# RG-LRU gates of a two-layer hybrid decoder: each inner gate tile reads two input tiles instead of three, one of them put together by ScalarE from the halves of two neighbours

## The reference, cut to what matters

```python
xb = xf.reshape(B, L, LRU_BLOCKS, LRU_BLOCK)                      # 16 blocks of 80
r = sigmoid(einsum('blnc,ncd->blnd', xb, w_a).reshape(B, L, W) + b_a)
i = sigmoid(einsum('blnc,ncd->blnd', xb, w_x).reshape(B, L, W) + b_x)
log_a = -LRU_C * r * softplus(-lam)
a = exp(log_a)
u = sqrt(-expm1(2.0 * log_a)) * (i * xf)                          # then h_t = a_t h_{t-1} + u_t
lru_branch = (gelu(y_lru) * hl) @ w_lru_out
```

## Time and profile before

| what | value |
|---|---|
| median of 3 runs | 2459.19 us (2458.72 to 2462.03) |
| the profiled execution's own time | 2456.01 us |
| span of its trace | 2454.2 us |
| TensorE busy | 2423.3 us, 99% of the span |
| VectorE, ScalarE, GpSimd busy | 1178.2, 645.1, 1634.4 us |
| LRU steps of the first layer | from 511.4 to 678.6 us of the span |
| the same steps of the second layer | 1211.9 us later |

### The profile page before, as it was taken

How to read it: one execution, slowest core, us unless ns; L and a number is a source line. 1 busy time by engine, 2 the same in 40 slices (tenths; PEclk the granted TensorE clock), 3 DMA queues, 4 the chain that set the end, 5 groups by cost and what they waited for, 6 DMA issues and landing times.

```text
span 2454.2 us, 53114 instructions
## 1 busy us (share of the span) xinstructions
PE 2423.3 (99%) x19640; PEld 2364.6 (96%) x19640; DVE 1178.2 (48%) x1587; ACT 645.1 (26%) x982; POOL 1634.4 (67%) x1685
## 2 busy tenths in 40 slices
PE   8999999999999999999999999999999999999998
PEld 7999999999999999999999999999999999999998
DVE  8646363678644432022266373736786454211223
ACT  2404040446811211011114041413666112100111
POOL 6464646578887776776765555555888776667765
PEclk9999999999999999999999999999999999999999
DMA  5636363522232222322257373645223232223222
GB/s 209 237 121 244 121 241 117 206 87 91 85 102 92 95 90 81 104 90 83 94 166 250 114 250 120 239 133 190 88 91 90 97 95 91 90 82 103 91 85 88
DMA packets 121737, 315.51 MB, mean 129 GB/s; under 512 B 12192, under 2 KB 12960, under 8 KB 121568
## 3 DMA queue, kind: packets, MB, share of 16 engines
q1 hardware_dynamic: 60480, 199.78, 25.5%
q10 hardware_dynamic: 61088, 113.34, 13.0%
HBM read 272.69 MB, written 40.38 MB: 128 GB/s over the span
## 4 chain that ended last, share of the span: by engine, by line
PE 91%; DVE 4%; DVEq 2%; ACT 1%; issue 1%; DMA 0%; ACTq 0%
PE proj L370 55%; PE aux L370 27%; PE aux L625 2%; DVE scratch L1126 2%; PE aux L582 1%; PE aux L555 1%; PE proj L633 1%; PE aux L633 1%; DVEq L1129 1%; DVE scratch L1184 1%; PE aux L611 1%; PE proj L625 0%; DVEq L807 0%; DVEq L1160 0%; DVEq L1187 0%
## 5 line engine op out<-in xcount | busy, mean ns | idle before, releaser
L358 POOL TENSOR_TENSOR w_low<-w_raw,w_high 128x512 fp32r<-128x512 f32 x840 | 1091.1, 1299 | 124.5 <-issue 2.1
L356 POOL TENSOR_SCALAR w_high<-w_raw 128x512 fp32r<-128x512 f32 x840 | 549.7, 654 | 674.1 <-PE proj L370 495.4
L370 PE MATMUL proj<-x_high,w_high 128*128 128x260 f32 x2752 | 558.8, 284 | 11.4 <-DVE x_low L797 11.0
L370 PE MATMUL proj<-x_high,w_low 128*128 128x260 f32 x2752 | 555.0, 283 | 0.0
L370 PE MATMUL proj<-x_low,w_high 128*128 128x260 f32 x2752 | 554.1, 283 | 0.0
L370 PEld LDWEIGHTS proj<-x_high,w_high 128*128 128x128 f32 x2752 | 425.3, 189 | 20.6 <-issue 16.9
L370 PEld LDWEIGHTS proj<-x_high,w_low 128*128 128x128 f32 x2752 | 424.8, 189 | 0.0
L370 PEld LDWEIGHTS proj<-x_low,w_high 128*128 128x128 f32 x2752 | 424.0, 189 | 0.0
L370 PE MATMUL proj<-split_scratch,w_high 128*128 128x260 f32 x2544 | 409.2, 283 | 0.0
L370 PEld LDWEIGHTS proj<-split_scratch,w_high 128*128 128x128 f32 x2544 | 348.6, 188 | 5.0 <-issue 5.0
L370 PE MATMUL aux<-x_high,w_high 128*128 128x260 f32 x1344 | 270.9, 283 | 0.0
(11 more groups left out here) (197 smaller groups left out, 2283.5 us busy)
## 6 DMA issues: line engine op xcount, KB each, us to landing
w_raw<-in_wstream SPq DMA_DIRECT2D x252, 512.0 KB, 3.5
scratch<-in_sret ACTq DMA_DIRECT2D x96, 512.0 KB, 6.9
out_ret_s<-scratch ACTq DMA_DIRECT2D x64, 512.0 KB, 4.4
w_raw<-in_wstream SPq DMA_DIRECT2D x72, 448.0 KB, 3.3
w_raw<-in_wstream SPq DMA_DIRECT2D x48, 384.0 KB, 3.0
scratch<-v_rows ACTq DMA_DIRECT2D x64, 256.0 KB, 3.9
w_raw<-in_wstream SPq DMA_DIRECT2D x48, 320.0 KB, 2.9
out_ret_p<-scratch ACTq DMA_DIRECT2D x8, 512.0 KB, 5.5
```

What stands on the lines that cost most here:

```text
L356: pool.tensor_scalar(WH[:, j, w], WR[:, j, w], 1.0, 0.0, ALU.mult, ALU.add)
L358: pool.tensor_tensor(WL[:, j, w], WR[:, j, w], WH[:, j, w].bitcast(F32), ALU.subtract).then_inc(s["w_split"], 1)
L370: m = pe.matmul(out, wt[:, w, blk * P:(blk + 1) * P], x[xi], start=first and n == 0, stop=last and n == 2)
```

## The change

The inner gate tiles (`t` = 1, 2, 3) read of their two neighbours only rows 64 to 127 of the tile before and rows 0 to 63 of the tile behind. The new kernel copies these two halves into one mixed tile, high and low part each, so that `gates(g,t)` reads two tiles: its own and the mixed one. The weights are laid out to match, and the unit of these steps has 6 blocks instead of 7. ScalarE makes the copies, 64 partitions by 520 columns each, in two calls a tile: `mix_below` (two copies of the upper halves) and `mix_above` (two of the lower halves, then the semaphore `mix_full`, on which TensorE now waits as well). In addition, the sigmoids of step (1,0) move ahead of three other steps on ScalarE, and `read_y(1,0)` on VectorE ahead of `conv_low(1,3)` and `conv(1,4)`.

```diff
-BAND = [sorted({(b * BLK + e) // P for b in range(t * P // BLK, (t * P + P - 1) // BLK + 1)
-                for e in (0, BLK - 1)}) for t in range(GT)]
+LAST_READ = [sorted({(b * BLK + e) // P for b in range(t * P // BLK, (t * P + P - 1) // BLK + 1)
+                     for e in (0, BLK - 1)})[-1] for t in range(GT)]
+MIXED = range(1, GT - 1)
+LOWER, UPPER = slice(0, P // 2), slice(P // 2, P)
+BAND = [(0, 1)] + [(t, "mix") for t in MIXED] + [(GT - 2, GT - 1)]
...
+        MIX = [[GL[1][i][:, GT - 1 - t % 2, :] for i in range(2)] for t in range(GT)]
...
                     q = 0
-                    pe.wait_ge(s["xc_low"], layer * LT + (g * GT + BAND[t][-1] + 1))
+                    pe.wait_ge(s["xc_low"], layer * LT + (g * GT + LAST_READ[t] + 1))
+                    if t in MIXED:
+                        pe.wait_ge(s["mix_full"], layer * (GROUPS * len(MIXED)) + (g * len(MIXED) + t))
                     for w in range(2):
...
-                        q = spread(ub0, u, YG_UNIT[t], ring_begin(layer, n + w), XCH, XCL, BAND[t], q)
+                        outs = ring_begin(layer, n + w)
+                        for k in BAND[t]:
+                            if q in (0, CUT):
+                                unit_begin(ub0, u, q // CUT)
+                            hi, lo = MIX[t] if k == "mix" else (XCH[:, k, :], XCL[:, k, :])
+                            m = product(outs, u % 2, q, [(hi[:, c * HALF:(c + 1) * HALF], lo[:, c * HALF:(c + 1) * HALF])
+                                                         for c in range(2)], k == BAND[t][0], k == BAND[t][-1])
+                            q += 1
+                        m.then_inc(s["r_done"], 1)
...
                 conv(1, 3)
+                read_y(1, 0)
                 conv_low(1, 3)
                 conv(1, 4)
...
-                    read_y(1, t)
+                    if t:
+                        read_y(1, t)
...
+                def mix_below(g, t):
+
+                    if t >= 3:
+                        r_done(LRU_TILE["y", g, t - 2] + 1)
+                    act.wait_ge(s["xc_low"], layer * LT + (g * GT + t))
+                    for i, src in enumerate((XCH, XCL)):
+                        A(MIX[t][i][UPPER, :], src[UPPER, t - 1, :].bitcast(F32), copy)
+
+                def mix_above(g, t):
+
+                    act.wait_ge(s["xc_low"], layer * LT + (g * GT + t + 2))
+                    for i, src in enumerate((XCH, XCL)):
+                        m = A(MIX[t][i][LOWER, :], src[LOWER, t + 1, :].bitcast(F32), copy)
+                    m.then_inc(s["mix_full"], 1)
...
                     A(LA[:, b, :], LA[:, b, :], ACT.Tanh, scale=CUR[:, PC_SP + c:PC_SP + c + 1]
                       ).then_inc(s["th_full"], 1)
+                    if t + 1 in MIXED:
+                        mix_above(g, t + 1)
                     act.wait_ge(*freed(layer, n + 2))
...
                 first_tap(0, 2)
+                mix_below(0, 1)
                 for t in range(GT):
...
                     gated_high(0, t)
+                    if t + 2 in MIXED:
+                        mix_below(0, t + 2)
+                gate_sigmoids(1, 0)
                 conv_high(*FILL_X[GT - 1])
                 first_tap(1, 3)
                 conv_high(1, 3)
                 first_tap(1, 4)
+                mix_below(1, 1)
                 for t in range(GT):
-                    gate_sigmoids(1, t)
+                    if t:
+                        gate_sigmoids(1, t)
+                        if t + 1 in MIXED:
+                            mix_below(1, t + 1)
```

More of the change, by code:

```diff
@@ L42 @@
 BLK = LW // NBLK
-BAND = [sorted({(b * BLK + e) // P for b in range(t * P // BLK, (t * P + P - 1) // BLK + 1)
-                for e in (0, BLK - 1)}) for t in range(GT)]
+LAST_READ = [sorted({(b * BLK + e) // P for b in range(t * P // BLK, (t * P + P - 1) // BLK + 1)
+                     for e in (0, BLK - 1)})[-1] for t in range(GT)]
+MIXED = range(1, GT - 1)
+LOWER, UPPER = slice(0, P // 2), slice(P // 2, P)
+for t in range(GT):
+    for row in {b * BLK + e for b in range(t * P // BLK, (t * P + P - 1) // BLK + 1) for e in range(BLK)}:
+        assert row // P == t or t not in MIXED or (row // P, row % P < P // 2) in ((t + 1, True), (t - 1, False))
+BAND = [(0, 1)] + [(t, "mix") for t in MIXED] + [(GT - 2, GT - 1)]
 QK, GATES = 2 * KT, VT
@@ L252, in build @@
         AUX = ctx.enter_context(nc.psum_tensor("aux", [P, 4, 512], F32))
[L254 removed]
+        names = ("mix_full go_pool setup_ld boot w_split w_used p_done t_free r_done "
                  "rope_done qk_high qk_low qz_full st_high st_low aux_mm kv_high kv_low "
@@ L1674, in weight_units, with rows_of @@
     n = 0
+    def rows_of(r):
+        if isinstance(r, int):
+            return np.arange(r * P, (r + 1) * P)
+        above, below = (r[1] + 1) * P, (r[1] - 1) * P
+        return np.concatenate([np.arange(above, above + P // 2), np.arange(below + P // 2, below + P)])
     def tile(w, col, rows, put=0):
         for i, r in enumerate(rows):
-            out[n, :, (put + i) * P:(put + i + 1) * P] = w[r * P:(r + 1) * P, col:col + P]
+            out[n, :, (put + i) * P:(put + i + 1) * P] = w[rows_of(r), col:col + P]
     def spread(size, tiles):
@@ L1737, in y_gates @@
                 gates.append(full)
-            spread(YG_UNIT[t], [(full, t * P, BAND[t]) for full in gates]
+            spread(YG_UNIT[t], [(full, t * P, [(k, t) if k == "mix" else k for k in BAND[t]]) for full in gates]
                    + [(w_in[l], off[5] + g * wide + t * P, range(MT))])
```

1 line of the change is left out of this document (removed).

## The result

The changed kernel takes 2462.8 us in the median of 12 runs (2461.41 to 2468.73); the kernel before, run beside it, 2458.88 us (2454.38 to 2462.52). The ratio is 1.0017, with a 95% interval of 1.0009 to 1.0025. So it is slower by 3.9 us: more than the uncertainty of this comparison, and less than the 4.9 us that the prediction drew as its line. The prediction said 2464.8 us. So the direction came as forecast, and the size falls on the other side of the prediction's own line, where its rival "nothing to measure" stands.

The account below looks back on a forecast made before the run. TensorE, busy 99%, was taken as the bound, with a slackless ScalarE-VectorE ring behind it. Each layer 3.3 us later less 0.5 relief, two layers 5.6 us, on 2459.2 gives 2464.8 us; range 2454 to 2471.

Parts of the forecast that it names:

- nothing to measure: Rival, chance 0.32: whole time within 0.2% (4.9 us), through copy pairs at 0.55 us or more gain on VectorE.
- The work removed: TensorE, both layers: 24 blocks, 17.3 us, and sigmoid stops, 5.6 us, go; the gain if nothing else were late.
- The price of a copy: ScalarE: a pair of 64-partition copies takes 1.18 us and puts off what follows by about 1.1 us.
- Group 0: First group's LRU steps: copies make the ring 2.2 us late; TensorE waits 1.0 us at gates(0,2), 3.0 at gates(0,3).
- The ring: LRU steps: ScalarE and VectorE release each other in turn, 16.3 us a step against TensorE's 15.87, without slack.
- The relief: VectorE gains 0.5 us a layer from lighter GpSimd work, bounds 0 and 3 us.
- The ring has no slack to give it back: Steps (0,3) and (0,4) hold no delaying pair, yet the 2.2 us of lateness was to stay.
- The turn: Start of group 1: gates(1,1) waits 7 to 9 us for mix_above(1,1), starting at 623.8; floor without VectorE lateness 621.6.
- Group 1: Second group's steps: ScalarE needs 13.0 us against TensorE's 12.3; gates(1,3) starts at 650.2 with slow matmuls, before 645.49.
- The clock: TensorE at half clock for 18 matmuls after the 7 to 9 us stop at gates(1,1): 1.9 us charged.
- The sum: Whole kernel: each layer 3.3 us later less 0.5, so 2.8; two layers 5.6 us slower.
- Faster: the ring gets ahead of today: Rival, chance 0.14: VectorE's conv(1,4) ends 1.1 to 1.7 us earlier through 2 to 4 us relief; about 2452 us.

Follow-up runs that it names:

- the shorter ring: Gelu and its table load left out of the LRU steps, in the changed kernel (2446.07 us) and in the kernel before (2452.33 us).
- the slots first: Kernel before with the moved sigmoids and read_y, plus both read_out of step (1,0) ahead of one_less_a2(1,0) on VectorE; no copies: 2453.09 us.
- group 1's mixed tiles and the slot sooner: Mixed tiles in group 1 alone, read_out(1) ahead of one_less_a2(1,0), and read_out(0) moved ahead of conv_low(1,4): 2451.46 us.
- group 1 early: Changed kernel with group 1's mix_above calls made early, right behind mix_below; group 0 as in the change: 2457.66 us.
- the moves alone: Kernel before with only the moved sigmoids and read_y(1,0); gates still over three tiles, no copies: 2465.43 us.
- mixed tiles in group 1 alone: Changed kernel with group 0 back on three tiles, group 1's lower copies early, both read_out of step (1,0) ahead of one_less_a2(1,0): 2451.36 us.
- mixed tiles and the slots first: Changed kernel with group 1's lower copies early and both read_out of step (1,0) ahead of one_less_a2(1,0): 2451.09 us.

## Why the prediction came out right, and where its steps did not

**The work removed** (24 blocks of 0.721 us) is right: 144 matmuls are gone. The stop of 2.8 us is gone too, in both layers. The sentence "If nothing else were late, this would be the gain" hid the main thing: before the change TensorE had 0.7 us to spare at the slot of `y(1,1)`. The prediction tied this gain to the order on ScalarE alone and overlooked VectorE's; with no copies and no wait the time was 2456.96, not near 2436. For the changed kernel itself this did not matter, since there the wait for the copies comes first.

**The price of a copy** is right: 1.15 us a pair against 1.18, so 64 partitions cost what 128 do.

**Group 0.** Waits of 0.63 and 3.58 us against 1.0 and 3.0. The ring was late as said: from the start of the stage, 0.88 us later after than before, `conv_high` of tile (0,4) stands at 554.76 against 552.14, so 1.7 us late by itself (said 2.2).

**The relief is the term that was mis-sized.** "The ring has no slack to give it back" failed at once: the next `conv_high` stood at 570.67 against 569.76, level again. Windows of 10 us behind `gates(0,3)`, before and after (us, busy of PE, PEld, DVE, ACT, POOL, then granted clock, DMA, GB/s):

```profile
559.10:569.10 10.00, 10.00 (x86) 10.00 (x85) 9.55 (x10) 5.30 (x10) 8.73 (x8) 1.00 0.26 82
```
```profile
560.00:570.00 10.00, 9.94 (x61) 9.97 (x61) 6.63 (x11) 7.94 (x12) 4.91 (x5) 0.70 0.14 41
```

While TensorE stands and then runs slowly, GpSimd works 4.9 us instead of 8.7, and VectorE's share from L1182 (now L1202) to the end of the convolution took 570.58 - 563.89 = 6.7 us against 569.67 - 560.24 = 9.4. So one pass gave back 2.7 us, against 0.5 for a whole layer, and inside the bound of 3. By the turn the forecast's 2.2 us of lateness were -0.6 in the first layer and +1.2 in the second (below): relief of 2.8 and 1.0.

The two layers are each other's control here. Up to `gates(0,3)` every `conv_high` has the same place in both stages within 0.02 us, and both have the stop of 3.58 us there. Behind it 26 matmuls of the first layer ran at the granted clock of 0.50, and 15 of the second. The same 10 us in the second layer, and VectorE's share there:

```profile
1773.28:1783.28 10.00, 9.94 (x70) 9.97 (x71) 6.79 (x10) 7.57 (x12) 5.74 (x6) 0.83 0.13 39
```
```profile
1777.17 0.70 DVE L1202 TENSOR_TENSOR scratch<-scratch 128x520 f32<-128x520 f32 x1 [2.86 <-ACT scratch L1613]
...
1781.47 3.89 DVE L1146 SCALAR_TENSOR_TENSOR scratch<-scratch,params_cur 128x509 f32<-128x509 f32 x3
```

GpSimd worked 5.74 us instead of 4.91, and VectorE took 1785.36 - 1777.17 = 8.2 us instead of 6.7: the layer in which TensorE was slow for longer is 1.5 us ahead at the next `conv_high`. So the half pace in group 0 is part of the relief, a link that the prediction did not have. That GpSimd's rest is what speeds VectorE up is borne out by the 840 convolution instructions above; that it is all of it is not shown.

**The turn.** `conv_high(1,4)` was forecast near 618 and came at 616.50 (616.18 in the earlier trace rows, so 0.6 early by itself), and `gates(1,1)` at 621.79 against 623.8, after 2.69 us and not 7 to 9. Set back by the 0.88 us this is 620.9, just under the 621 that I had named as the point where I am wrong, and 0.7 below the floor that held without lateness. In the second layer, 2.24 us later at the start of its stage, `conv_high(1,4)` stands at 1831.58, 1.2 us late by itself (before: 1828.1), the wait is 5.64 us, and `gates(1,1)` starts at 1836.88. The mechanism is that of the forecast, the second layer near its size, the first at a third. The layers part at the half pace behind `gates(0,3)`, as shown; why the clock treated the same stop in two ways, no run shows.

**Group 1.** Waits of 0.77 and 0.72 us in the first layer (forecast 0.7 each, as 13.0 less 12.3). `gates(1,3)` starts at 648.15, with the offset taken off 1.8 us later than the earlier trace rows where 4.7 was said.

**The clock** fell, but elsewhere. Windows after, behind `gates(0,3)`, at the turn, and in the second layer's:

```profile
560.00:564.00 4.00, 3.94 (x18) 3.97 (x19) 0.93 (x4) 3.96 (x7) 1.14 (x2) 0.50 0.16 30
564.00:568.00 4.00, 4.00 (x28) 4.00 (x27) 3.78 (x7) 1.99 (x5) 1.77 (x2) 0.75 0.19 72
...
621.80:626.00 4.20, 4.20 (x35) 4.20 (x36) 2.23 (x5) 4.14 (x5) 1.76 (x3) 1.00 0.30 88
...
1836.00:1840.00 4.00, 3.12 (x14) 3.15 (x15) 1.75 (x4) 3.95 (x5) 1.14 (x2) 0.50 0.03 6
```

A granted clock of 0.50 is 1.2 of 2.4 GHz. In the first layer it fell behind the 3.58 us stop at `gates(0,3)`, where I had charged nothing, and not at the turn. The cost, from 18 matmuls in 4 us and then 28 where 33.5 pass at full pace, is 1.85 + 0.66 = 2.5 us. In the second it fell twice, behind the 3.58 and the 5.64 us stop; the same reckoning over four windows gives 3.8, 1.4 and 2.4 (said 1.9 for the turn).

**The sum** was +5.6 us and is +3.9. The second layer's stage grew by 2.83 us, where 2.8 was said. That it is so near is luck: 0.5 us more relief than charged and 0.5 us more half pace behind the turn cancel. (The other 1.4 us of half pace and the waits of group 0 lie ahead of the turn and only shorten the stop there, to 5.6 us in place of 7 to 9.) The first layer's grew by 0.41: the relief was too small by 2.3, and no slow matmuls came at the turn. So the sum was right for one layer and far too high for the other. **The rivals:** "nothing to measure" had 0.32, one way to it being a relief of 2 us a layer, and 1.9 is the mean that came. With more half pace beside it the median fell between its 2461.5 and the forecast. In the LRU steps the clock stayed down no longer than 8 us anywhere, but fell three times instead of twice. "Faster: the ring gets ahead of today" was the right place to look: the shorter ring and the slots first show that there the gain is to be had, and this change does neither.

What stays open: the medians of the five fastest kernels with the Gelu are 6.1 to 8.9 us below before's, and their stages together only 3.9 to 5.7 us shorter. Before's profiled execution was 3.2 us below its median, and the granted clock of its other executions says in part why. Of the 63 that ran beside the experiments, 10 have a mean granted clock of 0.998, as the profiled one has, and a median of 2456.9 us; 25 have 0.997 and 2458.8; 25 have 0.996 and 2460.3. So most executions of before seem to lose time to the half clock that its trace does not show, and a comparison of medians can credit another kernel with more than the stages do. Where in the program the clock falls in those executions, one trace can't say.

## What to carry to other kernels

An engine that is busy 99% of the span can still be paced by a ring of two others that has no slack; before pricing removed work, look at each slot or semaphore that the busy engine takes next, when it was freed, and behind which wait the freeing instruction stands. A stop that is removed can come back at the next such place: here 2.80 us at the sigmoids became 4.22 at `read_out`. The cheap remedy was to put the slot's release ahead of that wait (2453.09 us, 6.9 below before, without mixed tiles); of all versions with the Gelu the lowest median is that with mixed tiles made early in group 1 besides (2451.09), though its interval overlaps that of the cheap remedy.

## What the runs showed of the hardware

VectorE's speed follows GpSimd's rests: the same three convolution instructions took 2.50 us where GpSimd stood 1.40 us of it, and 3.50 where it worked through. So a stop of TensorE, which lets GpSimd rest, speeds the engine up for which TensorE waits.

In the changed kernel the stops of 3.58 and 5.64 us were followed by half the pace, those of 0.63 to 2.69 us by the full one. But the 2.43 us of the kernel with group 1's mixed tiles and the slot sooner were followed by half the pace at once, while in the first layer behind 2.98 us (the changed kernel without Gelu), 3.33 us (group 1 early) and 4.22 us (the moves alone) it came only after 0.6 to 1 us. Even the same stop at the same place differs: in the kernel whose copies nobody waits for, 1.91 us at a slot of `read_y` in either layer, these are the 4 us behind it:

```profile
578.30:582.30 4.00, 4.00 (x33) 4.00 (x34) 2.07 (x3) 3.94 (x5) 3.10 (x4) 1.00 0.02 7
1792.56:1796.56 4.00, 4.00 (x20) 4.00 (x21) 2.06 (x3) 3.94 (x5) 2.82 (x4) 0.57 0.02 9
```

The granted clock was 1.00 in the first layer and 0.57 in the second, 33 matmuls against 20. A stop of 1.77 us (mixed tiles in group 1 alone) did the same: full pace in the first layer, half in the second. So the length of the stop alone does not sort these cases. The Trainium skill, "TensorE: Matmul & The Clock Gate", section "Why this matters for your kernels", warns of long idle gaps between bursts; the stops of 3.15 us and more, all followed by half the pace, agree with it, those of 1.77 and 1.91 us show that one about half as long can do it.

A slow TensorE need not lengthen the whole. In that same kernel the layer with the 20 slow matmuls is the shorter one, 156.56 us against 158.75, as in the changed kernel the layer with the longer half pace in group 0 is. Both times TensorE had to wait behind it anyway; that VectorE gained meanwhile by GpSimd's rest is the reading that fits, and was not tried by itself. It is no rule: with mixed tiles and the slots first the layer with the longer half pace in group 0 is the longer one, 154.95 against 154.46.

A ScalarE copy of 64 partitions by 520 columns takes 0.62 us (median of 48 in the changed kernel), about as long as one of 128 partitions (0.64).
